# Two mixer openings of a two-block fp32 kernel reordered: conditioning products, key norms, turned tiles and GpSimd's masks

## The reference

```python
y = concatenate([short_conv_mixer(p_conv, ...),
                 hgrn2_mixer(p_hg, lb_all[l], hgrn_norm[l]),
                 rwkv7_mixer(p_rw, mu, w0, w2, a0, a2, g2, k_k, k_a, r_k, ln_w, ln_b)], -1)
h = h + y @ w_mix_out[l]
```

## Time and profile before

| | |
|---|---|
| median of 3 runs | 3637.02 us (3633.15 to 3640.12) |
| the profiled execution | 3640.51 us, its span 3638.7 us |
| TensorE busy | 3392.3 us (93%) |
| VectorE busy | 2818.5 us (77%) |
| ScalarE, GpSimd busy | 1544.3 us, 706.9 us |
| mean granted TensorE clock | 0.967 |
| mixer of layer 0, from "mixer open" to the group norm | 300 to 494 us |

### The profile page before, as it was taken

The page is one execution under the profiler, slowest core; times in us unless marked ns, Lnnn a source line. Parts: engine busy times, 40 slices in busy tenths (PEclk is TensorE's granted clock), DMA queues, the critical chain, the costliest instruction groups (busy, mean ns, idle before and its releaser), DMA issues.

```text
span 3638.7 us, 53250 instructions
## 1 busy us (share of the span) xinstructions
PE 3392.3 (93%) x21102; PEld 2856.0 (78%) x21102; DVE 2818.5 (77%) x3245; ACT 1544.3 (42%) x2123; POOL 706.9 (19%) x457
## 2 busy tenths in 40 slices
PE   8997999999997999999788999999799789999996
PEld 8995789999995789997555777777686667777775
DVE  8886677888876677976758888888574688888884
ACT  1013132001023133011334888888431358888883
POOL 0000220101000120101001443443100023444430
PEclk9998999999998999999999999999899999999998
DMA  6545244454544334541035999999642269999993
GB/s 238 192 177 186 93 153 156 172 193 176 188 162 188 121 144 151 188 183 70 1 116 188 376 377 373 369 371 378 276 187 100 82 239 349 351 351 346 349 345 132
DMA packets 119853, 799.39 MB, mean 220 GB/s; under 512 B 33824, under 2 KB 35872, under 8 KB 49440
## 3 DMA queue, kind: packets, MB, share of 16 engines
q1 hardware_dynamic: 78480, 735.14, 54.3%
q0 software_dynamic: 39024, 59.61, 4.6%
q10 hardware_dynamic: 2080, 1.05, 0.1%
HBM read 808.77 MB, written 71.83 MB: 242 GB/s over the span
## 4 chain that ended last, share of the span: by engine, by line
PE 80%; DVE 14%; ACT 3%; DMA 1%; issue 1%; DVEq 0%; POOL 0%; ACTq 0%; SPq 0%; POOLq 0%
PE ps L452 76%; PE ps L466 4%; DVE ring_r L399 2%; DMA ring<-yd_dram 1%; DVE ring_r L398 1%; DVE ring_r L2805 1%; DVE arena L2249 1%; DVE ring_r L417 1%; DVE ring L1267 0%; ACT ring_r L411 0%; ACT arena L1740 0%; DVE arena L1180 0%; DVE mrow L2035 0%; ACT arena_hi L2869 0%; ACT arena L1447 0%
## 5 line engine op out<-in xcount | busy, mean ns | idle before, releaser
L452 PE MATMUL ps<-arena_r,ring_r 128*128 128x256 f32 (+1 forms) x9776 | 1273.7, 288 | 36.8 <-DVE ring_r L399 15.5
L452 PEld LDWEIGHTS ps<-arena_r,ring_r 128*128 128x128 f32 x9776 | 1212.8, 190 | 73.2 <-DVE ring_r L399 15.7
L452 PE MATMUL ps<-ring_r,arena_r 128*128 128x512 f32 (+1 forms) x2906 | 805.6, 392 | 5.6 <-DVE arena_r L2121 5.2
L452 PEld LDWEIGHTS ps<-ring_r,arena_r 128*128 128x128 f32 x2906 | 528.3, 189 | 117.2 <-DVE arena_r L2121 5.6
L452 PE MATMUL ps<-arena_hi,arena_r 128*128 128x512 f32 x1540 | 507.6, 397 | 4.7 <-DVE ring_r L2830 4.7
L399 DVE TENSOR_TENSOR ring_r<-ring,ring_r 128x4096 fp32r<-128x4096 f32 (+2 forms) x104 | 445.4, 4283 | 3.6
L2946 POOL DMA_INDIRECT yd_dram<-arena,small x129 | 228.3, 1770 | 731.3 <-PE ps L466 640.7
L452 PEld LDWEIGHTS ps<-arena_hi,arena_r 128*128 128x128 f32 x1540 | 290.0, 188 | 69.3 <-DVE ring_r L2830 5.1
L2805 DVE TENSOR_TENSOR ring_r<-ring,ring_r 128x2048 fp32r<-128x2048 f32 x130 | 298.0, 2292 | 22.4 <-ACT ring_r L2869 14.6
L2805 DVE TENSOR_TENSOR ring_r<-ring,arena_hi 128x2048 fp32r<-128x2048 f32 x128 | 293.5, 2293 | 24.3 <-ACT arena_hi L2869 17.5
L2938 POOL DMA_INDIRECT arena<-xd_dram,small x129 | 270.3, 2095 | 152.7 <-DVE arena L2628 62.1
(11 more groups left out here) (343 smaller groups left out, 3560.2 us busy)
## 6 DMA issues: line engine op xcount, KB each, us to landing
ring<-wexp_dram SPq DMA_DIRECT2D x387, 1024.0 KB, 8.4
ring<-stream_dram SPq DMA_DIRECT2D x143, 2048.0 KB, 7.7
ring<-yd_dram SPq DMA_DIRECT2D x7, 2048.0 KB, 11.9
arena<-yd_dram SPq DMA_DIRECT2D x5, 2048.0 KB, 9.3
xd_dram<-arena POOLq DMA_DIRECT2D x6, 512.0 KB, 6.3
consts_sb<-consts_dram SPq DMA_DIRECT2D x1, 2242.0 KB, 15.8
arena<-xd_dram,small POOLq DMA_INDIRECT x129, 10.5
yd_dram<-arena,small POOLq DMA_INDIRECT x129
```

The lines of the kernel that those rows point to most:

```text
L452: return pe.e.matmul(ps, lhsT=lhsT, rhs=rhs, start=start, stop=stop, skip_group_check=True)
```

## The change

In `weave`, which all four engines follow:

```diff
+            fill(2)
             piece("before")
-            fill(2)
+            piece("key norms")
             piece("scans")
             piece("query")
             piece("exps")
             piece("identities")
             level()
-            fill(2)
+            fill(4)
             piece("keys")
             piece("roots")
             piece("hats")
-            fill(3)
+            fill(2)
+            piece("hturned")
             piece("hgates")
+            piece("turned")
             level()
-            piece("hturned")
-            piece("turned")
-            fill(5)
             for g in range(3):
                 piece("first", g)
                 level()
                 fill(1)
```

The TensorE part of the old piece "roots" becomes the piece "key norms" (VectorE's part keeps its name and place):

```diff
-                if name == "roots":
+                if name == "key norms":
```

VectorE names the point "inverse", l, 1, g behind each group's first products, no longer behind all three and the levels between them:

```diff
                                                  v3(bank(*T)[:, 0:256], 128)).then_inc(*dve.mark("left", *T))
+                    dve.here("inverse", l, 1, i)
                 if name == "inverse":
-                    if i == 0:
-                        for g in range(3):
-                            dve.here("inverse", l, 1, g)
-                    else:
+                    if i:
                         second_product(*STEPS[i - 1])
```

GpSimd issues its masks accordingly, in the same sequence as before:

```diff
-                if name == "inverse":
-                    if i == 0:
-                        masked(*STEPS[0])
-                    if i + 1 < len(STEPS):
-                        masked(*STEPS[i + 1])
+                if name == "first":
+                    masked(*STEPS[i])
+                if name == "inverse" and i + 3 < len(STEPS):
+                    masked(*STEPS[i + 3])
```

## The result

The changed kernel has a median of 3646.05 us (3637.88 to 3655.49, 17 runs), the kernel before 3640.22 us (17 runs): ratio 1.0015, interval 1.0009 to 1.0022. A repeat gave 1.0014 (1.0005 to 1.0023). So it is slower by about 5 us, where the prediction had 2 us faster with a range that reached to both sides. The profiled execution took 3637.88 us, the fastest of the 17, with a span of 3636.1. A single execution of this kernel doesn't tell the sign: the slowest of the kernel before took 3646.17.

A forecast was written before the change was run, and what follows sets the result against it. TensorE, busy 93% of the span, was taken as the bound. Terms of -7.5, -4.8, +3.1, +6.0 and +2.2 gave -1.0 us a layer, -2.0 for two, so a 3635.0 us median; 8-in-10 range 3622 to 3648.

The forecast's parts named there:

- Opening, -7.5 a layer: Mixer opening up to VectorE's first L1267: it starts at about 327.5 instead of 335.04; -7.5 us, ends -6.0 to -8.5.
- To the second products, -4.8: From first L1267 to TensorE's first second product: masks come earlier, ScalarE's copy behind decays(5) is next bound; -4.8 us, or -4.0.
- The change doesn't do what it says: Rival on TensorE's 4.38 us wait: GpSimd's mask not its true end, 4 us a layer missing, 3643; no separate chance.
- Inverse, +3.1: Inverse: one more half-block and fold, 2.1 us, uncovered, and output transposes 1 us later; +3.1 us, +2.1 if that hides.
- State steps, +6.0: State steps: mo loads late, TensorE stands 3.9 us at fold(9), half clock until about 481; +6.0 us (+2.0 to +12.4).
- Group norm, +2.2: Group norm: GpSimd's low parts start later, so L1398 takes about 3.2 us instead of 0.97; +2.2 us (0 to 2.2).
- The sum: All five stage terms of a mixer layer together: -1.0 us a layer, -2.0 for two; ends -9.2 and +7.7 a layer.
- The dear-end rival: State steps: TensorE stands 3.9 us or more, all behind at half clock; +5.4 us a layer, 3647.8 us; chance 0.14.
- The clock in the opening: Opening rival: 24 transposes and first group's products at half clock, 3.6 us less won, +2.6 a layer, 3642; chance 0.10.

The follow-up runs named there:

- experiment 2: Kernel before, with only GpSimd's first three inverse masks formed behind each group's first products: ratio 0.9978, 7.65 us faster.
- experiment 5: Changed kernel with GpSimd's masks put back behind all three groups: 3656.39 us, ratio 1.0046 against the kernel before.
- experiment 7: Kernel before, with only hturned and turned moved ahead of level 1, fill calls unchanged: 3624.56 us, ratio 0.9961.
- experiment 8: Kernel before, with the turned tiles ahead of level 1 and masks behind each group, no fill piece moved: 3621.05 us, ratio 0.9950.
- experiment 9: Changed kernel with fill(0.78) for fill(0.75) in the inverse, so row 9's copy precedes the casts of mo: 3626.40 us, 0.9959 against the kernel before.
- experiment 3: Changed kernel with ScalarE's casts of mo placed behind the copy of row 9: 3632.40 us, ratio 0.9980 against the kernel before.
- experiment 12: Changed kernel with opening fill 2, 3, 3 (fold(0) behind the hats products) and fill(0.78) in the inverse: 3622.06 us, 0.9950 against the kernel before.
- experiment 10: Kernel before, with ScalarE's casts of mo moved ahead of the copy of row 9, no fill piece moved: 3676.73 us, ratio 1.0093.
- experiment 4: Changed kernel with fill(0.945) for fill(0.75) in the inverse, 28 pieces before the state steps: 3625.99 us, ratio 0.9966 against the kernel before.
- experiment 6: Changed kernel with fill(0.945) in the inverse and opening fill 2, 3, 3, fold(0) behind the hats products: 3623.26 us, 0.9954 against the kernel before.

## Why the prediction was wrong in its sign, point by point

- **Opening, -7.5 a layer:** measured -7.5, -7.0, -6.6 and -7.0 in four layers. The path was as told: the hats behind fold(0), fold(0) behind ScalarE's first row. TensorE's idle time there was 10.07 us in layer 0, not 7: the products in front of it ran at full clock (24 instructions in 2.76 us) and had begun 1.0 us sooner. That costs nothing more, as ScalarE's row sets the end.
- **To the second products, -4.8:** -4.77 and -4.79 by TensorE's rows (348.10 - 329.16 = 18.94 against 23.71), and ScalarE's copies behind decays(5) end the wait as predicted, 1.32 us in the row above. Experiments 2 and 5 confirm it from both sides (3.2 to 3.8 and 4.5 us). "The change doesn't do what it says" falls.
- **Inverse, +3.1:** +4.0, -1.6, +4.4 and +2.8 in the third column, mean 2.4. The sum treated a product piece as a fixed 1.04 us. Experiments 7 and 8 show this stage 5 us apart with no instruction of it changed, at a clock of 0.98 and 0.92.
- **State steps, +6.0, with bounds +2.0 to +12.4: this is the step that failed.** It measured +10.5, +13.3, +13.6 and +7.1, mean 11.1. The mechanism was the predicted one, its place and its releaser too; the size was wrong. TensorE stood 4.57 to 4.85 us and not 3.9; in layer 0 the load of mo took 9.5 us from its issue at 454.11 to the cast, not 8.7. Behind the row the prediction has 15.4 us to the group norm (474.3 to 489.7); layer 0 took 18.8 (468.71 to 487.55) and layer 1 22.1. Two terms in that were too small. The first is the half clock. I let it last some 7 us behind the stand and then end for good, as in the openings of the earlier trace rows. So it went in one of four layers (7.3 us at half clock, +7.1 in all). In the layer shown above it ended after 8.3 us, but fell again in the y products, which took 5.5 us instead of 4.0 (+10.5). In the other two it lasted past the start of the group norm and the y products took 7.7 (+13.3 and +13.6). The second is the pair L716 and L720: 0.9 us in the sum, 2.1 to 2.6 measured. The sum has a slip the other way, too: its own terms, with half clock until 481, give 489.1 and +5.3, not 489.7 and +6.0.
- **Group norm, +2.2:** -0.1, -1.2, -1.2 and +1.7. By the prediction's own times the low parts end near 498 and L1398 starts at 498.9, behind them, so the +2.2 didn't follow from them. In the first profile's layer 0 GpSimd's last low part ended at 496.1, and the counterpart of L1398 started at 496.7 and took 0.96 us; in the one layer with +1.7 it did start beside a low part, and took 2.73. By the Trainium skill ("SBUF — State Buffer", Who interferes with whom) a VectorE instruction with two SBUF inputs contends with a GpSimd instruction that reads SBUF, as the two share a port pair under "an exclusive lock". The trace agrees: L1391 started at 490.83 inside a low part that ran from 489.92 to 493.05, and took 3.04 us; an instruction of the same size behind GpSimd's end took 0.96.
- **The sum:** with the measured means it is -7.0 - 4.8 + 2.4 + 11.1 - 0.2 = +1.5 a layer, +3 in all, near the measured 4 to 6. The two gains were sized to 0.5 us and the inverse to 0.7 on average; the sign hung on the tail. The prediction says that the tail decides against the change from 9.2 us a layer on; state steps and group norm together measured 10.9. The dear-end rival, which had 0.14, was nearer the truth (3647.8 us, measured 3646.05) than the forecast of 3635.0.
- **The clock in the opening** as a rival: it didn't come. In layer 0 the 24 transposes took 2.84 us, 0.12 each, right behind a product piece at full clock. In the other three openings the piece in front still took 1.88 us, at half clock, and the transposes took 2.88 to 3.03, so the clock was full again from their start on. The rule of the Trainium skill on transposes ("TensorE: Matmul & The Clock Gate", Part 4: PE-mode transpose) didn't come into play; whether it holds, no run here shows.

## What to carry to other kernels

When work is moved away from a place, follow what its end releases: here a piece four places later freed a ring slot later, and on a strictly ordered engine the wait for that load stood ahead of the one small copy that the bound engine needed next. A queue order in which that copy comes first took one fill step (experiment 9), and made the changed kernel the faster one. Removing the stand took most of the price away: state steps and group norm together stood 10.9 us a layer above before with it and 2.6 without it (means of the changed kernel's four layers and of the six of experiments 3, 9 and 12). A stand of TensorE in this stretch cost about twice its length: 17.1 us of it in both layers cost 36 in experiment 10. Judge edits of a few us in such a kernel by medians, as one execution can be off by the whole effect.

## What the runs showed that I had not expected

- **The same instructions take 4.2 or 7.0 us behind the same wait.** In TensorE's timelines of kernels 7 and 8, the attended values' 36 small products come after a wait of 1.45 us for the same VectorE line, and the clock falls in one and not in the other:

```profile
416.78 4.20 PE L452 MATMUL ps<-arena 128*128 128x64 f32 x36 [1.45 <-DVE arena L1223]
420.82 2.90 PE L452 MATMUL ps<-ring 128*128 128x128 f32 x24
```

```profile
408.71 7.02 PE L452 MATMUL ps<-arena 128*128 128x64 f32 x36 [1.45 <-DVE arena L1223]
415.53 5.00 PE L452 MATMUL ps<-ring 128*128 128x128 f32 x24
```

  That is 4.9 us over the two rows, and all of the difference between their inverses (79.3 and 84.1 us). What decides it stays open.
- **The price of more products can't be read from one profile.** With three more product pieces and two folds in each inverse than before, 5 us of work at full clock, the stage took 86.0 us in experiment 4 (clock 0.96) and 91.3 and 91.0 in experiment 6 (0.91), against 84.2 before and 79.3 for the same instructions as before in experiment 7.
- **Whether the gains add can't be told.** The turned tiles alone gave 16 us, the masks alone 7.7, both 19.6. The missing 4 us lie within the intervals (9 to 19, 4 to 11 and 13 to 23 us). The profiles show the turned tiles' inverse at 79.3 and that of both at 84.1, but the mean clocks of their five executions hardly differ (0.967 to 0.971 and 0.969 to 0.971).
